# Entering a chunked recurrence without common waits, and splitting an output product around its end

## The chip, the cores and the metric

The kernel runs on one core of a Trainium2 chip. Its engines are TensorE (PE, matrix products; PEld is its weight load), VectorE (DVE), ScalarE (ACT), GpSimd (POOL) and SyncE (SP, which here only issues DMAs). Each has its own instruction stream, ordered by hand; streams meet through semaphores. The metric is the device time of one execution in microseconds (us), median of the runs; a kernel's profile comes from one further execution.

## The reference

Two blocks run one after the other on x (512 tokens x 1024 channels, fp32).

- **First block (RWKV-7).** x is normalised; six token-shifted mixes of it are multiplied by `w_in` into r, k, v, the gate g and two low-rank inputs. For each of 16 heads of width 64 a 64x64 state runs over the tokens: `S = S*w + (S @ -kk) (kk*a)^T + v k^T`, `y = S @ r`. y is normalised by head (mean and variance over 64), scaled, gets the bonus `sum(r*k*r_k) * v`, is multiplied by silu(g) and by `w_out`, and x is added: x1.
- **Second block.** Three vectors (shift, scale, gate) are computed from a condition by `w_ada` (1024 x 3072), for x and for a context of 256 tokens. x1 is normalised and modulated; products with `w_in_2` give a Fourier part and neighbourhood attention (8 heads, with the context's keys and values); both are gated, joined, multiplied by `w_out_2`, scaled and added to x1.

## The kernel before

The first block is computed in stages on PE. **Projections**: k, r, then a loop over eight channel tiles c (w, a and v, with the decays made on DVE and ACT), then eight products for g, `("g", c)`, each 24 matmuls of the split kind (three products of rounded halves, lines 518 to 520). **Recurrence**: tokens are cut in chunks of 64 (e = 0..7) and the channel tiles in two halves (hb = 0, 1); the 16 pairs in `ORDER` are the groups g = 0..15. One iteration of the loop over g works on several groups at once: `off_product` and `grow` double the inverted blocks of group g+1 and g (L679, L662 to L696), `turned` transposes (L662), `gram` makes the products of group g+2 (L647), `rhs_values`, `from_state`, `scan_sa` and `scan_out` (L708, L726, L742/L748, L760/L768) carry the state. Beside them stand the modulation's matrix-vector products with `w_ada` (`mods_here`: L780, L790), and from g = 9 the transposes of finished token tiles (`turn_y`: L807; each token tile j of 128 tokens has four pieces).

Before the recurrence, 16x16 diagonal blocks are inverted by forward substitution on DVE. `first_l` makes their products on PE, ACT copies them out (`copy_l`) and stores them in DRAM, `fetch_blocks(q)` (L1260) reads them back in another layout, `solve(b, part)` on DVE (L1601 to L1617; b = 0, 1; six parts of growing size) inverts, `store_inverse(b)` (ACT's queue, L1265) stores, and `fetch_inverse(b)` (SP's queue, L1120, eight DMAs) reads back; POOL's `expand(g)` (L2007) spreads them.

In the kernel before, DVE does all of both solves after the loop over c, with one buffer `XO` for both, so that the second waits for the store of the first. `gate(0)` to `gate(5)` (L1597, they free the banks of g) stand between the solve's parts, then `mask_gram(0)`, `gate(6)`, `gate(7)`. Then DVE, ACT and POOL each wait for the two others (`others_done`, `dve_phase` and so on) since the recurrence's buffers lie where the stage before had its own. PE does all eight g products, `gram(0)`, the first modulation product (whose bank 3 held g 7 and is freed by `gate(7)`), and the loop.

After the loop comes **y**: for each token tile j, DVE takes the mean off (`centre`, L1704 to L1706), ACT squares, DVE sums (L1757), ACT takes the root, DVE scales (L1760, L1761), PE transposes (`turn_y`), ACT applies the scale (`take_y`, L1350), DVE adds the bonus and gates (`finish_y`, L1713, L1715, which count up `y_gated`). PE then computes `project_y(t, h)` (token tile t, output half h; L524, 32 matmul records, two accumulations of 256 columns each). In order: tile 2's transposes, projections (0..2, 0), tile 3's transposes, (3, 0), (0, 1), the context's transposes (L896), (1, 1), (2, 1), x1's transposes for tile 0 (`turn_x1`, L879), (3, 1), tile 1's, and then the context's keys (first L524 after it).

On SP's queue, weights go through three buffers: block n is fetched when block n-3 is used. `fetch_inverse(0)` stands before block `split_g + 8`, `fetch_inverse(1)` before `split_g + 11`; x again (2 MB), the last block of `w_out` and the context follow when the recurrence has ended (L1142 to L1145; the context waits also for all of `y_gated`).

Lines that the steps touch: 

```
L524   last = mm(o, lhs(k), rhs(k), ...)          # accumulate
L780   last = mm(banks[MODS_BANK][...], SILC[:, k, :], w[:, k, :], ...)
L1613  own.own(TT(tmp, xo[...], LTB[b][...], MUL)) # solve
L1979  TT(WLO[...], WR[...], WHI[...], SUB)        # POOL splits a block of g's weights
```

## Time and profile before

| | us |
|---|---|
| median of 3 runs | 823.29 (821.58 to 829.12) |
| profiled execution | 819.92 |
| its span | 818.0 |
| PE busy | 762.1 (93%) |
| DVE, ACT, POOL busy | 446.0, 306.6, 172.3 |
| mean granted TensorE clock | 0.971 of full speed |

The span is the profile's own clock; about 1.9 us of the execution's time lie outside of it. In the page's second part each digit is a fortieth of the span (20.45 us). The granted clock has two levels, full (2.4 GHz) and half (1.2 GHz); a digit or figure between them is a mean over time.

### The profile page before, as it was taken

The page shows a single profiled execution, that of the slowest core. Times are in us where ns is not written, and L with a number is a line of the kernel's source. Part 1 is how long each engine was busy: PE and PEld are TensorE (multiplying, and loading weights), DVE is VectorE, ACT ScalarE, POOL GpSimd, SP SyncE. Part 2 cuts the span into 40 slices and gives each one's busy share as a digit, 9 for nine tenths or more (in the row PEclk, how much of TensorE's full clock was granted, in tenths as well). Part 3 has the DMA queues.
Part 4 walks back from the last instruction along what each step waited for, and adds up shares of the span by engine and source line. Part 5 has one row for each costly group of instructions (what it writes and reads, how often), then busy time and mean ns, then how long its engine had stood idle before and what let it go on. Part 6 is the DMA issues. An engine that isn't in the chain of part 4 may idle for free.

```text
span 818.0 us, 17638 instructions
## 1 busy us (share of the span) xinstructions
PE 762.1 (93%) x7612; PEld 618.4 (76%) x7612; DVE 446.0 (55%) x800; ACT 306.6 (37%) x638; POOL 172.3 (21%) x133
## 2 busy tenths in 40 slices
PE   3999999999998998988859899999999999999997
PEld 3588887777786787877847788877777777775697
DVE  5944635777879233556544123749655666754611
ACT  5534445566531122334331235523225453424200
POOL 2334330000342212324210000740000000002642
PEclk9999999999999599999978899999999999999999
DMA  7133233224458663310031134213302111231131
GB/s 245 30 100 103 78 100 107 78 79 91 123 126 217 141 220 125 128 55 4 4 121 35 52 103 112 62 53 92 113 3 76 52 53 53 62 107 52 51 105 52
DMA packets 116765, 72.83 MB, mean 89 GB/s; under 512 B 26832, under 2 KB 114128, under 8 KB 116688
## 3 DMA queue, kind: packets, MB, share of 16 engines
q1 hardware_dynamic: 98496, 65.12, 27.0%
q10 hardware_dynamic: 18192, 6.58, 3.3%
q8 instruction: 61, 1.00, 0.5%
q14 instruction: 16, 0.13, 0.1%
HBM read 64.35 MB, written 7.34 MB: 88 GB/s over the span
## 4 chain that ended last, share of the span: by engine, by line
PE 83%; DVE 9%; issue 3%; ACT 2%; DMA 2%; POOLq 0%; POOL 0%; SPq 0%; ACTq 0%; DVEq 0%
PE bank L524 21%; PE bank L983 9%; PE bank L518 6%; PE bank L520 6%; PE bank L519 6%; PE bank L647 2%; PE bank L1024 2%; PE bank L1007 2%; DVE arena L1613 2%; PE bank L780 2%; PE bank L696 2%; PE bank L543 2%; PE bank L679 2%; PE bank L1103 2%; PE bank L1105 2%
## 5 line engine op out<-in xcount | busy, mean ns | idle before, releaser
L524 PE MATMUL bank<-arena 128*128 128x256 f32 (+1 forms) x768 | 182.6, 396 | 4.5 <-DVE arena L1715 3.1
L524 PEld LDWEIGHTS bank<-arena 128*128 128x128 f32 x768 | 147.1, 194 | 38.4 <-issue 16.0
L1979 POOL TENSOR_TENSOR w_lo<-arena,w_hi 128x1024 fp32r<-128x1024 f32 x24 | 58.1, 2419 | 179.7 <-ACT w_hi L1196 179.7
L1196 ACT ACTIVATE w_hi<-arena 128x1024 fp32r<-128x1024 f32 x44 | 46.4, 1057 | 86.3 <-DMA arena<-w_in 84.6
L518 PE MATMUL bank<-x_hi,w_hi 128*128 128x512 f32 x192 | 76.4, 398 | 0.0
L520 PE MATMUL bank<-x_hi,w_lo 128*128 128x512 f32 x192 | 75.6, 394 | 0.0
L519 PE MATMUL bank<-x_lo,w_hi 128*128 128x512 f32 x192 | 75.3, 392 | 0.0
L518 PEld LDWEIGHTS bank<-x_hi,w_hi 128*128 128x128 f32 x192 | 36.1, 188 | 8.7 <-issue 0.8
L520 PEld LDWEIGHTS bank<-x_hi,w_lo 128*128 128x128 f32 x192 | 36.0, 188 | 8.4
L2076 POOL COPY arena<-arena 128x512 f32<-128x512 f32 x4 | 2.5, 614 | 189.2 <-DVE arena L1889 189.2
L519 PEld LDWEIGHTS bank<-x_lo,w_hi 128*128 128x128 f32 x192 | 36.1, 188 | 8.0
L983 PE MATMUL bank<-xn_hi,w_hi 128*128 128x512 f32 x96 | 39.6, 413 | 0.0
L983 PE MATMUL bank<-xn_hi,w_lo 128*128 128x512 f32 x96 | 38.0, 395 | 0.0
L983 PE MATMUL bank<-xn_lo,w_hi 128*128 128x512 f32 x96 | 37.9, 395 | 0.0
L1103 PE MATMUL bank<-w_out_hi,mix_hi 128*128 128x256 f32 x128 | 36.6, 286 | 0.2 <-DVE mix_lo L1946 0.2
L2007 POOL TENSOR_TENSOR arena<-arena 128x512 f32<-128x512 f32 x16 | 21.0, 1318 | 71.9 <-PE bank L742 56.1
L1557 DVE TENSOR_TENSOR x_lo<-arena,x_hi 128x512 fp32r<-128x512 f32 x24 | 21.6, 900 | 26.6 <-ACT x_hi L1200 26.5
L1105 PE MATMUL bank<-w_out_hi,mix_lo 128*128 128x256 f32 x128 | 36.0, 282 | 0.0
L1104 PE MATMUL bank<-w_out_lo,mix_hi 128*128 128x256 f32 x128 | 35.9, 281 | 0.0
L1868 DVE TENSOR_REDUCE arena<-bank 128x1 f32<-128x256 f32 x32 | 13.6, 424 | 40.0 <-PE bank L1000 40.0
L1489 ACT ACTIVATE arena<-arena 128x256 f32<-128x256 f32 x32 | 16.3, 509 | 50.8 <-DVE arena L1872 50.2
L1806 DVE TENSOR_TENSOR w_lo<-arena,w_hi 128x1024 fp32r<-128x1024 f32 x20 | 25.6, 1283 | 16.6 <-ACT w_hi L1196 16.6
(252 smaller groups left out, 1636.6 us busy)
## 6 DMA issues: line engine op xcount, KB each, us to landing
arena<-w_in SPq DMA_DIRECT2D x45, 512.0 KB, 3.9
arena<-w_ada SPq DMA_DIRECT2D x12, 1024.0 KB, 5.1
arena<-w_in SPq DMA_DIRECT2D x8, 1024.0 KB, 5.4
arena<-w_out SPq DMA_DIRECT2D x8, 1024.0 KB, 5.1
lt_dram<-arena ACTq DMA_DIRECT2D x16, 256.0 KB, 2.3
arena<-x SPq DMA_DIRECT2D x4, 512.0 KB, 5.6
arena<-x SPq DMA_DIRECT2D x1, 2048.0 KB, 7.6
out<-arena SPq DMA_DIRECT2D x8, 256.0 KB, 2.1
```

The source lines that it names most:

```text
L518: mm(o[:, :], w_hi[:, wk], x_hi, start=(k == 0), stop=False)
L519: mm(o[:, :], w_hi[:, wk], x_lo, start=False, stop=False)
L520: return mm(o[:, :], w_lo[:, wk], x_hi, start=False, stop=(k == KT - 1))
L524: last = mm(o, lhs(k), rhs(k), start=(k == 0), stop=(k == n - 1))
L983: last = mm(banks[5 + i % 2][:, :], w[slot][:, k * P:(k + 1) * P], v[k][:, :], start=(r == 0), stop=(r == 3 * KT - 1))
L1103: mm(oi, MXHI[k][:, at], W2HI[nb][:, wk], start=(k == 4), stop=False)
L1104: mm(oi, MXHI[k][:, at], W2LO[slot][:, wk], start=False, stop=False)
L1105: last = mm(oi, MXLO[k][:, at], W2HI[nb][:, wk], start=False, stop=(k == 3))
L1196: A(WHI[n % 3][:, :], WR[n % 3][:, 0:1024], ACT.Copy).then_inc(weights_rounded, 1)
L1557: TT(XLO[m][c][:, :], MIXES[m][:, c, :], XHI[m][c][:, :].bitcast(f32), SUB).then_inc(mixed, 1)
L1806: TT(WLO[n % 3][:, :], WR[n % 3][:, 0:1024], WHI[n % 3][:, :].bitcast(f32), SUB)\
L1979: TT(WLO[n % 3][:, :], WR[n % 3][:, 0:1024], WHI[n % 3][:, :].bitcast(f32), SUB)\
```

## The change

The three common waits go. g's products 6 and 7 get fixed banks (6 and 1) and `gram(0)` stands after product 5, `gram(1)` after product 6; the first modulation product moves into the loop. Groups 0 and 1 get `GM` buffers, and group 0 an `XS` buffer, in places that are free earlier (`GMG`, `XSG`), and each solve its own `XO` and `XTMP`. Parts 0 and 1 of `solve(0)` move into iterations 6 and 7 of the loop over c, with the fetch of the blocks one iteration earlier; the rest is put in a new order with the gates, and the stores and fetches of the inverses move with it.

At the other end, `project_y` is called by halves (t, h, i) of 16 matmul records. (0,0,0), (0,0,1) and (0,1,0) run in iterations 15, 16 and 17 of the loop, which now ends at 17 instead of 20. Tile 2's transposes come after it, in four banks instead of one; the projections before tile 3's transposes are (1,0), (1,1,0) and (2,0). The orders of ACT and DVE follow: tile 3's statistics go between tile 2's last steps, and x1's right halves are made before the context's norm. SP fetches the context without waiting for `y_gated`.

```diff
-        XO = arena[:, xi0 + 2560:xi0 + 3584].rearrange("p (q s a b) -> p q s a b", q=2, s=2, a=BLK)
-        XTMP = arena[:, xi0 + 3584:xi0 + 4096]
+        gt_at = xi0 + 4096
+        XO = [arena[:, at:at + 1024].rearrange("p (q s a b) -> p q s a b", q=2, s=2, a=BLK) for at in (gt_at + 3072, xi0 + 2560)]
+        XTMP = [arena[:, at:at + 512] for at in (gt_at + 2560, xi0 + 3584)]
...
+        XSG = [ROOT[0].rearrange("p (s c n) -> p s c n", s=2, c=4)] + [XS[:, g % 4] for g in range(1, GROUPS)]
+        GMG = [arena[:, at:at + 1024].rearrange("p (h c n) -> p h c n", h=2, c=4) for at in (lts_at, lts_at + 1024)] +\
+            [GM[g % 4] for g in range(2, GROUPS)]
...
-        def others_done(eng, n, mine):
-
-            for s in (act_phase, dve_phase, pool_phase):
-                if s is not mine:
-                    eng.wait_ge(s, n)
...
-                if i == 0 and g:
-                    pe.wait_ge(rhs_copied, g)
+                if i == 0:
+                    pe.wait_ge(rhs_copied, g) if g else stored(pe, ("g", 6))
...
+                o = out_bank((name, j, h), 3 if j < 2 else ((3, 0, 1, 2), (1, 2, 7, 4))[j - 2][piece])
...
-            gram(0)
-            mods_here(-1, 0)
+            for c in range(KT):
+                lo, hi = split_weights()
+                o = next_bank(("g", c)) if c < 6 else out_bank(("g", c), (6, 1)[c - 6])
+                for k in range(KT):
+                    if c == 0:
+                        pe.wait_ge(mixed, KT * 3 + k + 1)
+                    last = split_product(o, lo, hi, XLO[5][k][:, :], XHI[5][k][:, :], k)
+                full(last, ("g", c))
+                if c == 5:
+                    pe.wait_ge(kappa_ready, KT)
+                if c in (5, 6):
+                    gram(c - 5)
             for b in range(8):
-                if b not in (4, 5, MODS_BANK) and uses[b]:
+                if b not in (1, 4, 5, 6, MODS_BANK) and uses[b]:
                     pe.wait_ge(bank_free[b], uses[b])
+            wo = []
+            OUT_BANKS = {(0, 0): 4, (0, 1): 5, (1, 0): 6, (1, 1): 3, (2, 0): 0, (3, 0): 6}
+
+            def project_y(t, h, i):
+
+                pe.wait_ge(y_gated, 2 * (t + 1))
+                if not wo:
+                    wo.extend([weights() for _ in range(3)] + [WX])
+                if (h, i) == (1, 1):
+                    pe.wait_ge(wx_here, 16)
+                if i == 0:
+                    out_bank(("o", t, h), OUT_BANKS[t, h]) if (t, h) in OUT_BANKS else next_bank(("o", t, h))
+                b = where["o", t, h][0]
+                last = accumulate(banks[b][:, i * 256:(i + 1) * 256], lambda k: YG[t][:, k, :],
+                                  lambda k: wo[2 * h + i][:, k, :])
+                if i:
+                    last.then_inc(bank_full[b], 1)
+
             pe.wait_ge(y_zeroed, 1)
-            for g in range(-1, GROUPS + 5):
+            for g in range(-1, GROUPS + 2):
...
+                if g == GROUPS + 1:
+                    project_y(0, 1, 0)
...
+                if g in (GROUPS - 1, GROUPS):
+                    project_y(0, 0, g - GROUPS + 1)
...
-                if g + 2 < GROUPS:
+                if 0 <= g < GROUPS - 2:
...
-            for t in range(3):
-                project_y(t, 0)
+            for piece in range(4):
+                turn_y(2, piece)
+            for t, h, i in ((1, 0, 0), (1, 0, 1), (1, 1, 0), (2, 0, 0), (2, 0, 1)):
+                project_y(t, h, i)
             for piece in range(4):
                 turn_y(3, piece)
-            project_y(3, 0)
-            block_key[taken[0] - 2] = block_key[taken[0] - 1] = ("o", 3, 0)
-            project_y(0, 1)
+            for t, h, i in ((0, 1, 1), (1, 1, 1), (3, 0, 0), (3, 0, 1)):
+                project_y(t, h, i)
+            block_key[taken[0] - 3] = block_key[taken[0] - 2] = ("o", 3, 0)
+            turn[0] = 0
...
-            project_y(1, 1)
-            project_y(2, 1)
+            for i in range(2):
+                project_y(2, 1, i)
             turn_x1(0)
-            project_y(3, 1)
+            turn_x1(1)
+            for i in range(2):
+                project_y(3, 1, i)
             block_key[taken[0] - 1] = ("o", 3, 1)
-            turn_x1(1)
...
-                if n == split_g + KT + 3:
+                if n == split_g + KT + 1:
...
-                    sp.wait_ge(y_gated, 2 * NT)
...
-                if c in (5, 6):
-                    fetch_blocks(c - 5)
+                if c in (4, 5):
+                    fetch_blocks(c - 4)
...
-                if c == 3:
-                    store_inverse(0)
-            A(CST[:, 0:1], CST[:, 4:5], ACT.Copy).then_inc(act_phase, 1)
-            store_inverse(1)
-
-            others_done(act, 1, act_phase)
+                if c in (1, 4):
+                    store_inverse(c // 4)
...
+            square_y(3)
+            take_y(2, 0)
+            root_y(3)
+            take_y(2, 1)
...
-                    if b:
-                        dve.wait_ge(inv_out, 16 * b)
...
+                if c >= 6:
+                    solve(0, c - 6)
...
-            for b in range(2):
-                for part in range(6):
-                    solve(b, part)
-                    if part in (1, 2, 4):
-                        gate(3 * b + (1, 2, 4).index(part))
             def mask_gram(g, h):
                 o = arrived(dve, ("gram", g, h)).rearrange("p (c n) -> p c n", c=4)
-                free(TT(GM[g % 4][:, h], o, gram_mask.unsqueeze(1).broadcast_to([P, 4, 2 * CH]), MUL), ("gram", g, h))
-
-            for h in range(2):
-                mask_gram(0, h)
-            gate(6)
-            gate(7)
+                free(TT(GMG[g][:, h], o, gram_mask.unsqueeze(1).broadcast_to([P, 4, 2 * CH]), MUL), ("gram", g, h))
+
             free(nc.vector.tensor_copy(BON, arrived(dve, "bonus")[:, 0:64]), "bonus")
-            nc.vector.tensor_copy(CST[:, 1:2], CST[:, 5:6]).then_inc(dve_phase, 1)
-
-            others_done(dve, 1, dve_phase)
+            for part in range(2, 5):
+                solve(0, part)
+            gate(0)
+            solve(0, 5)
+            gate(1)
+            for i in range(3):
+                solve(1, 2 * i)
+                solve(1, 2 * i + 1)
+                gate(2 + i)
+            gate(5)
+            dve.wait_ge(inv_out[0], 16)
+            for i in range(2):
+                for h in range(2):
+                    mask_gram(i, h)
+                gate(6 + i)
...
+            centre(3)
+            finish_y(2, 0)
+            sum_y(3)
+            finish_y(2, 1)
+            norm_y(3)
...
-            make_x1(0, 1)
-            for t in range(1, NT):
+            norm_x1(0)
+            norm_x1(1)
+            make_x1(3, 0)
+            for t in (2, 3):
                 make_x1(t, 1)
-                norm_x1(t - 1)
-            norm_x1(NT - 1)
+                norm_x1(t)
...
+            arrived(pool, "bonus")
+            expand(0)
+            stored(pool, ("g", 6))
+            nc.gpsimd.memset(YL, 0.0).then_inc(y_zeroed, 1)
             arrived(pool, ("g", KT - 1))
-            expand(0)
-            others_done(pool, 1, pool_phase)
-            arrived(pool, "bonus")
-            nc.gpsimd.memset(YL, 0.0).then_inc(y_zeroed, 1)
```

## Rows read from the trace of the kernel before

**Rows 1.** The page, second part: granted clock of PE, in tenths.

```profile
PEclk9999999999999599999978899999999999999999
```

**Rows 2.** Busy time by stretch: us, each engine's busy (instructions), clock, DMA share, GB/s.

```profile
216.00:262.00 46.00, 45.67 (x224) 36.45 (x222) 39.20 (x72) 13.16 (x19) 18.46 (x9) 1.00 0.70 165
262.00:294.80 32.80, 27.64 (x528) 21.75 (x528) 10.88 (x27) 4.54 (x13) 7.68 (x10) 0.69 0.71 193
294.80:304.60 9.80, 9.27 (x284) 7.75 (x280) 3.04 (x8) 2.95 (x8) 2.08 (x3) 1.00 0.68 217
410.00:420.00 10.00, 6.67 (x137) 5.73 (x136) 4.00 (x8) 5.35 (x14) 0.39 (x1) 0.74 0.01 2
420.00:434.00 14.00, 6.59 (x37) 4.75 (x36) 6.06 (x7) 3.73 (x10) 3.05 (x3) 0.62 0.64 226
434.00:455.00 21.00, 21.00 (x96) 18.29 (x95) 7.41 (x10) 1.37 (x2) 0.00 (x0) 0.97 0.00 0
455.00:460.00 5.00, 1.91 (x17) 1.67 (x15) 3.43 (x5) 2.90 (x8) 0.00 (x0) 0.93 0.00 0
460.00:467.00 7.00, 6.97 (x18) 5.66 (x19) 0.00 (x0) 1.42 (x3) 0.00 (x0) 0.56 0.47 152
467.00:501.00 34.00, 34.00 (x174) 30.19 (x173) 6.43 (x12) 12.06 (x28) 0.00 (x0) 1.00 0.19 62
```

**Rows 3.** Timeline of PE at the entry: start, us, line; in brackets idle before, releaser.

```profile
260.57 1.10 PE L647 MATMUL bank<-arena 64*64 64x128 f32 x32
265.53 1.94 PE L780 MATMUL bank<-arena 128*32 128x256 f32 x16 [3.86 <-DVE arena L1597]
```

**Rows 4.** Timeline of DVE before the entry (start, us).

```profile
222.55 0.26 DVE L1615 TENSOR_REDUCE arena<-arena 128x14 f32<-128x98 f32 x1
...
232.39 2.63 DVE L1613 TENSOR_TENSOR arena<-arena 128x338 f32<-128x338 f32 x1
...
244.51 0.48 DVE L1607 MEMSET arena<- 128x512 f32 x1 [3.10 <-DMA inv_dram<-arena]
...
257.02 0.77 DVE L1613 TENSOR_TENSOR arena<-arena 128x338 f32<-128x338 f32 x1
...
265.44 0.14 DVE L1663 COPY arena<-arena 128x1 f32<-128x1 f32 x1
```

**Rows 5.** Timeline of POOL in the same stretch.

```profile
232.00 2.40 POOL L1979 TENSOR_TENSOR w_lo<-arena,w_hi 128x1024 fp32r<-128x1024 f32 x1 [1.74 <-ACT w_hi L1196]
```

**Rows 6.** Timeline of DVE at the head of iterations 6 and 7 over c.

```profile
195.86 0.43 DVE L1622 TENSOR_SCALAR arena<-arena 128x512 f32<-128x512 f32 x1 [2.33 <-ACT arena L1271]
...
206.91 2.19 DVE L1622 TENSOR_SCALAR arena<-arena 128x512 f32<-128x512 f32 x1 [3.10 <-ACT arena L1271]
```

**Rows 7.** Line 1260 (fetch of the blocks), issue of the first.

```profile
191.16 0.41 ACTq L1260 DMA_DIRECT2D arena<-lt_dram  x1
```

**Rows 8.** DMA issues of the whole span: count, KB each, us to landing (median).

```profile
arena<-w_ada SPq DMA_DIRECT2D x12, 1024.0 KB, 5.1
arena<-lt_dram ACTq DMA_DIRECT2D x4, 128.0 KB, 4.9
arena<-x SPq DMA_DIRECT2D x1, 2048.0 KB, 7.6
```

**Rows 9.** Timeline of SP at the entry: the second inverse's eight fetches.

```profile
267.39 6.91 SPq L1120 DMA_DIRECT2D arena<-inv_dram  x8
```

**Rows 10.** Timeline of PE at the recurrence's end and after it.

```profile
411.98 0.65 PE L696 MATMUL bank<-arena 64*64 64x32 f32 x16 [1.93 <-DVE arena L1673]
...
460.03 17.06 PE L524 MATMUL bank<-arena 128*128 128x256 f32 x64 [3.13 <-DVE arena L1715]
...
501.15 7.07 PE L524 MATMUL bank<-arena 128*128 128x256 f32 x32
```

**Rows 11.** Timeline of DVE at the recurrence's end: tiles 2 and 3, scaling.

```profile
422.29 2.64 DVE L1761 TENSOR_TENSOR arena<-arena 128x1024 f32<-128x1024 f32 x1
...
440.53 1.23 DVE L1761 TENSOR_TENSOR arena<-arena 128x1024 f32<-128x1024 f32 x1
```

More of the change, by code:

```diff
@@ L625, in _ @@
             first_l(KT - 1)
-            for c in range(KT):
-                lo, hi = split_weights()
-                o = next_bank(("g", c))
-                for k in range(KT):
-                    if c == 0:
-                        pe.wait_ge(mixed, KT * 3 + k + 1)
-                    last = split_product(o, lo, hi, XLO[5][k][:, :], XHI[5][k][:, :], k)
-                full(last, ("g", c))
-            pe.wait_ge(kappa_ready, KT)
             def gram(g):
@@ L1352, in take_y @@
                 free(ins, ("yT", j, h))
-            for g in range(-1, GROUPS + 5):
+            for g in range(-1, GROUPS + 2):
                 nxt, old = g + 1 < GROUPS, 0 < g <= GROUPS
@@ L1729, in _, with sum_y, norm_y @@
             heads_of = lambda a: a.rearrange("p (h n) -> p h n", n=HD)
-            for g in range(-1, GROUPS + 5):
+            def sum_y(j):
+                dve.wait_ge(gn_squared, j + 1)
+                nc.vector.tensor_reduce(stat(1, j), heads_of(SQ), AX.X, ADD).then_inc(gn_sums, 1)
+            def norm_y(j):
+                dve.wait_ge(gn_root, j + 1)
+                own.own(nc.vector.reciprocal(stat(2, j), stat(2, j)))
+                TT(heads_of(YT[j]), heads_of(YT[j]), bc(stat(2, j)), MUL).then_inc(y_normed, 1)
+            for g in range(-1, GROUPS + 1):
                 now, nxt, old = 0 <= g < GROUPS, g + 1 < GROUPS, 0 < g <= GROUPS
```

107 lines of the change are left out of this document (44 added, 63 removed).

## The prediction

> **What bounds the kernel.** The page comes first: PE is busy for 93% of the span, and its granted clock is full except in two places, the fourteenth fortieth (266 to 286 us) and the twenty-first to twenty-third (409 to 470) [rows 1]. These are the two ends of the recurrence, where the change works. The busy time by stretch says what they cost [rows 2]. Busy time times the granted clock is the time the same work would take at full clock. From 262.0 to 294.8, the first iterations, that is 27.64 x 0.69 = 19.1 us in 32.8. From 410 to 501 it is 4.9 + 4.1 + 20.4 + 1.8 + 3.9 + 34.0 = 69.1 us in 91. So 13.7 and 21.9 us are lost, part as idle time, part as half clock.
>
> Then the timelines, for what ends the waits. At the entry PE ends `gram(0)` at 261.7 and starts the first modulation product at 265.53; that takes 1.94 us, which is the half level. It waited 3.86 us for line 1597, the last `gate` on DVE [rows 3]. DVE is busy or waiting for its own store until 265.44 [rows 4], while PE was dense from 216 to 262 at full clock (45.67 of 46) [rows 2]. So DVE sets the entry, not the common waits: the others were done. At the other end PE waits 1.93 us before 411.98 and 3.13 before 460.03, each time for DVE, and within 420 to 434 it is busy for less than half [rows 2, 10].
>
> **The entry, part by part.** *DVE's load.* From 216.4, its first memset, to 265.4 DVE needs 49 us. It is busy for 39.2 of them up to 262 [rows 2] and for the 3.4 after. Two parts of `solve(0)` leave; part 1 ends with the reduce at 222.55 [rows 4], so they lasted 6.4 us. `mask_gram(1)` comes in (two of about 0.65). The store wait (3.10) goes, since each solve has its own `XO` [rows 4]. That makes 39.2 + 3.4 - 6.4 + 1.3 = 37.5 us: DVE could be ready at 254. But gates 6 and 7 need PE's last products, which end at about 257.5 and 263, so DVE has some 9 us in hand at g's last product, and from now on PE sets the time.
>
> *PE's stream.* Until 262 nothing of it is removed; `gram(1)`, which takes 1.10 us [rows 3], moves ahead of the loop. g 0 to 5 fill banks 2, 3, 4, 5, 0, 1, so `gram(0)` after product 5 needs gates 2 and 3 alone, due on DVE at about 243, when PE wants them at 250. `mask_gram(0)`, due about 255, is wanted by `gram(1)` at 257. The last gate falls at about 264.8, while PE is in `turned(0)` and the modulation product; `grow(0)` wants DVE at 265.4. PE should never pause for more than half a microsecond, so the clock stays full.
>
> *Its gain.* The work of 262.0 to 294.8 is 19.1 us at full clock. With the small waits of an iteration at full clock (9.27 busy of 9.80) [rows 2] it takes 20.2. **Gain 12.6 us**; I count 12.
>
> *What is moved to DVE's loop over c.* Part 0 and part 1 of `solve(0)`, about 2.7 and 1.7 us when nothing disturbs them, stand at the heads of iterations 6 and 7, where DVE waited for ACT for 2.33 and 3.10 us [rows 6]. Iteration 6 gets 0.4 us later, PE is on work that DVE gave it an iteration before. The blocks must have landed: the first fetch was issued at 191.16 in iteration 5 [rows 7] and would be in 4, the second in 5 at that place; 4.9 us to landing [rows 8] gives 196.1, where DVE arrives at 193.5 and spends 0.6 on memsets first. It may wait up to 2 us, on an iteration of 11 (195.86 to 206.91 [rows 6]). Between 0 and 2 us on PE; I take 0.3.
>
> *Queues.* SP issues the eight fetches of an inverse in 6.91 us [rows 9]. The second inverse now stands before the second modulation block. If it is solved at about 252 and stored by 255, SP is free at 262, and that block lands 5.1 us later [rows 8], at 267.5; PE wants it at about 268.5. Between 0 and 2 us, taken as 0, since the third block has more time.
>
> *A rule against it.* A solve step of 338 columns took 2.63 us at 232.39, and 0.77 at 257.02 when POOL was idle; a POOL split started at 232.00 and took 2.40 [rows 4, 5]. Eight such splits lie beside the solves, so DVE's budget above, which has the measured times, holds some 10 us of this already. The Trainium skill, "SBUF — State Buffer", "Who interferes with whom", says that the two engines share a pair of ports as an exclusive lock and the second fully blocks. The trace agrees; by that rule the moved parts can be hit too, which would add one split, 2.4 us, to DVE.
>
> **The exit.** All work from 410 to 501 is 69.1 us at full clock. The change does not remove any; it fills the recurrence's gaps. Walked through in the old time: (0,0,0) covers 410.0 to 413.5, when DVE's `mask_z` (due 411.9) and ACT's copy are awaited; (0,0,1) and (0,1,0) do the same for iterations 16 and 17, which end at 425.6 instead of 421.6. Tile 2's transposes have been ready since 419 and take 2.4 us in four banks. (1,0) and (1,1,0) then run to 438.4. Meanwhile tile 3 is centred (from 426), and tile 2 taken and finished: y_gated for (2,0) falls at about 437.3, only 1 us ahead. Tile 3 is scaled by 438.8 and PE turns it at 445.3. (0,1,1), (1,1,1) cover ACT's and DVE's last steps. x, `w_out`'s last block and the context, 4 MB, are asked for at 426; x alone takes 7.6 us [rows 8], all about 15; ACT needs the context by 443. `turn_x1` 0 and 1 have their norms ready before 470. The context's keys, at 501.15 before [rows 10], would start at 479.3. **Gain 21.9 us** at best. From it I take 2.5: handovers with margins of 1 to 4 us stand at (2,0), at tile 3's transposes and at the context, and the scaling of tile 2 took 2.64 us beside a POOL operation against 1.23 for tile 3 [rows 11]. **Net 19.4.**
>
> After 501 all engines keep their order, and the stage moves as a block; between 294.8 and 410 too.
>
> **Sum.** 819.92 - 12 + 0.3 - 19.4 = 788.8 us for a profiled execution. That execution was 3.4 us below the median of the three runs; half of this is put on top: **790**.
>
> **The rivals.**
>
> *DVE's chain stays late (0.14).* If locks and fetches cost DVE over 9 us more, `gram(1)` or the loop's first step pauses, and after a pause the clock was half from about 264.7 to 289 [rows 2]. For it: DVE is at 39.2 of 46 already. Against: the slack of 9. The entry then gives only about 3: 798 to 799.
>
> *The exit has a new pause (0.16).* (2,0) or tile 3 comes 2 us late; the clock falls as after the wait of 3.13 at 460.03 (0.56 for 7 us [rows 2], 3.1 us lost) or as at 415 to 434. Cost 5 to 9: 795 to 799. With the one before (0.02): 805.
>
> *Slower: half clock through the recurrence (0.04).* PE goes straight from dense products to many short ones with small waits. The first stretch needed 32.8 us for 19.1 of work, 1.72 to 1; at full clock it is 9.80 to 9.27, 1.06 to 1 [rows 2]. An iteration of 9.8 us would grow by 6.1. After five of them the gain of 31 is gone; from the seventh the kernel is slower by over 1%; all thirteen from 294.8 give about 868. Against: the same iterations ran at 1.00 with waits like these. The Trainium skill, "TensorE: Matmul & The Clock Gate", "A second HAM failure mode: psum-queue depth-cycling", tells of such a case, short pauses between groups of matmuls that make the clock swing; the trace has no swing in 294.8 to 304.6, and rule and rival would give the same time.
>
> *It does not do what it says (0.03).* The fills in the recurrence lengthen its own chain one for one, and the entry stays bound by DVE: 815 to 823.
>
> **Numbers.** The forecast holds with 0.61; its own range is 784 to 795. The full range is 782 to 805. About 1% (8 us) is what a measurement of this kernel can tell from none. Faster by more: 0.92 (0.61 + 0.14 + 0.16 + 0.02, less 0.01 for still larger pauses). Within 1%: 0.04 (these and the last rival). Slower: 0.04.
>
> **What would show it.** Entry: no PE wait over 1 us between 255 and 275, modulation products at half of 1.94 us from the first, iteration 2 begun at about 283 instead of 294.8; DVE's memset of `solve(1)` without a wait. Exit: three blocks of 16 L524 records among L726 and L742; clock 1.00 from 405 to 470 (old time); keys' first L524 20 to 22 us before the old distance. It would be wrong if the clock row shows a digit under 8 at either end, if DVE's waits at the heads of iterations 6 and 7 turn into waits for the fetch that reach PE, or if PE waits for ACT's `take_y` before (2,0).

## The result, and the profile after

The changed kernel takes 795.08 us in the median of four runs (794.85 to 796.46), the kernel before 822.43 on the same chip (821.36 to 829.12). The ratio is 0.969 (95% interval 0.965 to 0.973). The forecast was 790 us, in a range of 782 to 805. The profiled execution took 794.85 us, its span is 793.0 against 818.0: 25.0 us less where 31.1 were forecast (819.92 to 788.8).

The page comes first: the totals of PE and the row of the granted clock, the answer to [rows 1].

```profile
PE 754.0 (95%) x7612; PEld 610.9 (77%) x7612; DVE 442.4 (56%) x799; ACT 306.3 (39%) x637; POOL 171.2 (22%) x132
PEclk9999999999999889899999999999999999999999
```

The 5 at the fourteenth fortieth has become two digits of 8, and the digits 7, 8 and 8 at the recurrence's end are gone. A third 8, at the seventeenth (317 to 337 us), was a 9 before. Then the busy time by stretch, the answer to [rows 2] (same columns).

```profile
216.00:262.00 46.00, 44.38 (x246) 35.34 (x245) 40.73 (x64) 12.70 (x17) 18.71 (x9) 1.00 0.70 156
262.00:285.00 23.00, 22.16 (x427) 16.91 (x426) 4.60 (x13) 4.50 (x12) 5.39 (x7) 0.78 0.92 249
...
420.00:434.00 14.00, 14.00 (x87) 12.28 (x86) 6.56 (x9) 4.54 (x11) 2.90 (x3) 1.00 0.75 273
434.00:455.00 21.00, 21.00 (x107) 18.63 (x106) 10.74 (x19) 8.39 (x19) 0.00 (x0) 1.00 0.05 19
```

The exit is what was forecast and better: no idle time and full clock. The entry is not: 1.6 us idle ahead of 262, and a clock of 0.78 up to 285. PE's timeline at the entry shows where (idle time before an instruction and its releaser in brackets), against [rows 3]:

```profile
258.26 1.10 PE L635 MATMUL bank<-arena 64*64 64x128 f32 x32 [1.62 <-DVE arena L1660]
...
266.16 1.07 PE L770 MATMUL bank<-arena 128*32 128x256 f32 x16
...
268.98 1.06 PE L667 MATMUL bank<-arena 64*64 64x32 f32 x30 [0.68 <-DVE arena L1694]
...
271.29 1.89 PE L770 MATMUL bank<-arena 128*32 128x256 f32 x16 [0.16 <-DMA arena<-w_ada]
...
289.16 0.25 PE L667 MATMUL bank<-arena 64*64 64x32 f32 x2
```

Iteration -1 begins at 265.08, `gram(1)` waits 1.62 us for the first mask, the first modulation product has full clock (1.07 us), that at 271.29 has half (1.89). Iteration 2 begins at 289.16, forecast at 283, before at 294.81. ACT's timeline says what `gram(1)` waited for.

```profile
254.65 1.06 ACT L1203 ACTIVATE w_hi<-arena 128x1024 fp32r<-128x1024 f32 x1 [9.75 <-DVE arena L1625]
```

DVE's timeline of the same kernel, against [rows 4, 6]:

```profile
196.25 0.16 DVE L1621 TENSOR_TENSOR arena<-arena 128x2 f32<-128x2 f32 x1 [2.03 <-DMA arena<-lt_dram]
...
233.50 0.48 DVE L1615 MEMSET arena<- 128x512 f32 x1
...
253.57 0.64 DVE L1625 COPY arena<-arena 128x512 f32<-128x512 f32 x1
...
256.23 0.69 DVE L1607 SCALAR_TENSOR_TENSOR arena<-arena,bank 128x512 f32<-128x512 f32 x1 [1.43 <-ACT arena L1309]
256.83 1.28 DVE L1660 TENSOR_TENSOR arena<-bank,arena 128x512 f32<-128x512 f32 x2
```

The second solve begins without a wait (233.50; before, 3.10 us of it) and ends at 254.2, where "about 252" was forecast. ACT had stood 9.75 us in the wait for exactly this, ahead of its store of the inverse. Behind that wait stood the rounding of g's last weights and the tanh of gate 5, for which DVE then waited 1.43 us before the first mask. The SP queue, against [rows 9]:

```profile
259.39 6.04 SPq L1128 DMA_DIRECT2D arena<-inv_dram  x8
265.47 33.98 SPq L1144 DMA_DIRECT2D arena<-w_ada  x9
```

The second modulation block is asked for at 265.47, behind the eight fetches. At the other end, PE's timeline against [rows 10]:

```profile
406.44 3.72 PE L522 MATMUL bank<-arena 128*128 128x256 f32 x16
...
413.59 3.72 PE L522 MATMUL bank<-arena 128*128 128x256 f32 x16
...
418.36 3.62 PE L522 MATMUL bank<-arena 128*128 128x256 f32 x16
```

And DVE's two scalings, against [rows 11]:

```profile
414.11 1.23 DVE L1749 TENSOR_TENSOR arena<-arena 128x1024 f32<-128x1024 f32 x1
...
434.39 1.22 DVE L1749 TENSOR_TENSOR arena<-arena 128x1024 f32<-128x1024 f32 x1
```

The three halves of `project_y` stand as blocks of 16 records between the recurrence's last steps, and no record from 406 to 476 us has a wait in brackets. Both scalings take 1.2 us.

**Four stretches.** Every trace can be cut at three places: the start of iteration 2; the last `off_product` (L667, before L679); the first split product of the second block's keys (L516, before L518). For the changed kernel, the answer for L667 (first and last start, us):

```profile
L667 PE MATMUL bank<-arena x512: 211/219/313, 265.1 to 404.6; 64*64 64x32 f32 x171
```

Its first split product of the keys starts at 512.3.

All kernels of this study, cut in this way (us; the first column is the stretch up to iteration 2):

| kernel | to iteration 2 | middle | exit | rest | span |
|---|---|---|---|---|---|
| before | 294.8 | 113.3 | 130.9 | 279.0 | 818.0 |
| changed | 289.2 | 115.4 | 107.7 | 280.7 | 793.0 |
| e1 exit only | 295.9 | 116.2 | 107.7 | 279.0 | 798.8 |
| e2 entry only | 289.2 | 114.8 | 129.6 | 279.0 | 812.6 |
| e3 common waits back | 290.8 | 114.5 | 107.7 | 279.0 | 792.0 |
| e4 store wait back | 293.3 | 115.5 | 107.7 | 280.7 | 797.2 |
| e5 changed again | 292.6 | 115.2 | 107.7 | 280.7 | 796.2 |
| e6 store later | 290.9 | 120.3 | 107.7 | 279.0 | 797.8 |
| e7 filler | 291.4 | 121.3 | 107.7 | 279.1 | 799.5 |
| e8 both | 292.0 | 120.3 | 107.7 | 279.0 | 799.0 |
| e9 fetch later | 290.1 | 114.5 | 107.7 | 279.0 | 791.3 |
| e10 and filler | 291.6 | 118.6 | 107.7 | 280.7 | 798.6 |
| e11 and blocks later | 294.6 | 116.3 | 107.7 | 279.0 | 797.6 |
| e12 all four | 293.2 | 115.1 | 107.7 | 280.8 | 796.8 |

So the 25.0 us are 5.6 from the entry and 23.2 from the exit, less 2.1 in the middle and 1.7 in the rest. Each row is one execution, and some are quicker than their kernel's median: the traced execution of e2 took 814.54 us, 5.8 less than e2's median, that of e3 3.0 less. The stretches tell where a trace spends its time; what a kernel takes is told by the medians below.

### The profile page after: what moved, and what is told of

Same layout as the page of the kernel before. It is cut to its first block, busy times and chain, and to the rows that moved or that the text cites. A ratio compares the mean times of both kernels' runs of the same rounds, so it can differ in the third digit from the quotient of the medians.

```text
span 793.0 us, 17638 instructions
## 1 busy us (share of the span) xinstructions
PE 754.0 (95%) x7612; PEld 610.9 (77%) x7612; DVE 442.4 (56%) x799; ACT 306.3 (39%) x637; POOL 171.2 (22%) x132
## 4 chain that ended last, share of the span: by engine, by line
PE 83%; DVE 9%; DMA 3%; issue 3%; ACT 1%; SPq 1%; POOLq 0%; POOL 0%; ACTq 0%; DVEq 0%
PE bank L522 20%; PE bank L991 9%; PE bank L516 6%; PE bank L518 6%; PE bank L517 6%; DVE arena L1621 3%; PE bank L1032 2%; PE bank L1015 2%; PE bank L635 2%; PE bank L770 2%; PE bank L541 2%; PE bank L684 2%; PE bank L1111 2%; PE bank L1113 2%; PE bank L1112 2%
## 5 line engine op out<-in xcount | busy, mean ns | idle before, releaser
L522 PE MATMUL bank<-arena 128*128 128x256 f32 (+1 forms) x768 | 180.7, 393 | 1.4 <-DVE arena L1878 1.4
L522 PEld LDWEIGHTS bank<-arena 128*128 128x128 f32 x768 | 144.5, 191 | 35.0 <-issue 17.1
L516 PE MATMUL bank<-x_hi,w_hi 128*128 128x512 f32 x192 | 76.6, 399 | 0.0
L518 PE MATMUL bank<-x_hi,w_lo 128*128 128x512 f32 x192 | 75.6, 393 | 0.0
L516 PEld LDWEIGHTS bank<-x_hi,w_hi 128*128 128x128 f32 x192 | 36.1, 188 | 9.0 <-issue 1.2
L518 PEld LDWEIGHTS bank<-x_hi,w_lo 128*128 128x128 f32 x192 | 36.0, 188 | 8.3
L1820 DVE RECIPROCAL arena<-arena 128x512 f32<-128x512 f32 (+1 forms) x12 | 33.8, 2816 | 1.1 <-ACT arena L1438 1.0
```

The source lines that it names most:

```text
L516: mm(o[:, :], w_hi[:, wk], x_hi, start=(k == 0), stop=False)
L518: return mm(o[:, :], w_lo[:, wk], x_hi, start=False, stop=(k == KT - 1))
L522: last = mm(o, lhs(k), rhs(k), start=(k == 0), stop=(k == n - 1))
L1820: own.own(nc.vector.reciprocal(r, r))
```

## The experiments

Three groups of four, each on one chip beside the kernel before; the changed kernel's 0.969 is from a group of its own. The kernel before had a median of 825.41 us beside e1 to e4, 825.14 beside e5 to e8 and 822.73 beside e9 to e12; a ratio is to that.

### One half of the change at a time

**e1, exit only.** The entry of before, and of the diff the calls of `project_y` by halves and what belongs to them:

```diff
+                if g == GROUPS + 1:
+                    project_y(0, 1, 0)
...
+                if g in (GROUPS - 1, GROUPS):
+                    project_y(0, 0, g - GROUPS + 1)
```

> The kernel before with the second half of the change alone (the first block's output product in halves around the recurrence's end, loop ended at GROUPS + 1), the entry as before. My theory: the two halves of the change simply add, and the exit is worth what the two traces show between the end of the last state's reading and the keys' first product, 22.3 us, less about 0.9 us that comes back behind it: 21.4 us less than before, about 801 us, ratio 0.974, and from 20 us before the keys' first product back to the recurrence the clock at 1.00. Rival: part of the gain hangs on the entry's state (the banks or the clock that it leaves), then less than 18 us, over 804 us.

Measured: 802.01 us, ratio 0.973 (0.969 to 0.976). The exit takes 107.7 us, as in the changed kernel.

**e2, entry only.** The other hunks of the diff; the bank counter is set so that the exit finds its old banks.

```diff
+            turn[0] = (turn[0] + 2) % 6
             pe.wait_ge(y_zeroed, 1)
-            for g in range(-1, GROUPS + 2):
+            for g in range(-1, GROUPS + 5):
```

> The changed entry alone, with the exit as before. My theory: iteration 2 begins 5 to 6 us earlier, the recurrence gives some 2 us of it back (half clock in 317 to 322 us), so 3.6 us less than before, about 819 us, ratio 0.9956. Rival, my prediction as it stands on record: 12 us, 810 us, ratio 0.985. Second rival: the 2 us are given back for a reason that has nothing to do with the entry (then they are missing here, 5.6 us less, 0.993).

Measured: 820.38 us, ratio 0.994 (0.992 to 0.996); iteration 2 at 289.2, as in the changed kernel. The same stretch of PE in e1 (us, PE busy, clock, DMA share, GB/s):

```profile
405.00:460.00 55.00, 53.71 (x599) 1.00 0.22 78
```

And in e2:

```profile
405.00:460.00 55.00, 41.02 (x317) 0.81 0.22 74
```

What follows: the halves add, as far as can be told. 0.973 x 0.994 = 0.967, the whole has 0.969 (0.965 to 0.973). My number of 12 us for the entry is refuted: the entry alone gives 0.6%, some 5 us.

### Did the common waits cost anything?

**e3.** `others_done` returns on the three engines, nothing is moved back.

```diff
             expand(0)
+            others_done(pool, 1, pool_phase)
             stored(pool, ("g", 6))
             nc.gpsimd.memset(YL, 0.0).then_inc(y_zeroed, 1)
```

> The changed kernel with the three common waits put back where the engines stand (ACT behind the last gate's tanh, DVE behind gate 7, POOL behind the expansion of group 0), all other moves kept. Theory A: the waits themselves had a price, by the one that they put on POOL: its clear of YL starts at 259.34 us in the changed kernel and would have to wait for DVE's gate 7, which ends at 266.5; PE's loop waits for that clear and could start only at about 267.3 instead of 265.08, ACT's first copy of the turned keys 0.3 us later: 2 to 4 us slower than the changed kernel, 797 to 799 us, ratio to before 0.969 to 0.972. Theory B: the moves (Gram products between the gate's last products, solves spread into the loop over c) are all that counts, and the waits are free: under 0.5 us, ratio as the changed kernel's.

Measured: 796.85 us, ratio 0.966 (0.961 to 0.971); that can't be told from the changed kernel's 0.969. The trace has the mechanism, with its size. POOL's timeline in e3:

```profile
265.94 0.52 POOL L2071 MEMSET arena<- 128x512 f32 x1 [7.11 <-DVE arena L1687]
```

PE's:

```profile
266.79 0.60 PE L674 MATMUL bank<-arena 64*64 64x32 f32 x14 [2.37 <-issue]
```

POOL's clear waits for DVE's last gate, PE for the clear, 2.37 us. Iteration 2 begins 1.6 us later than in the changed kernel, although the whole stage stands 0.9 us earlier in e3 (PE's last block of L582, L589 in e3, starts at 212.79 against 213.73); counted from there it is 2.5 us, within theory A's 2 to 4. In the whole that is no more than what the middle and the rest differ by from trace to trace. So taking the waits out is worth about 2.4 us in the place where they stood, and the total doesn't show it.

### Has DVE slack?

**e4.**

```diff
                 if part == 0:
+                    if b:
+                        dve.wait_ge(inv_out[0], 16)
                     own.own(nc.vector.memset(xo, 0.0))
```

> The changed kernel in which DVE waits for the first inverse's store again before it begins the second solve (the second buffer stays, only the wait returns). It tests the slack of some 9 us that my prediction gave DVE between the second solve and the Gram masks. The store is issued at 232.9 us and such stores take 4.5, so DVE would stand from 233.5 to 237.4. Theory A (no slack: the solve's end holds ACT in its store wait, then the gates, the masks and PE): the loop starts 2 to 4 us later (2 if one of the three lock collisions beside POOL's splits, of 2.2 us each, falls into the wait), 797 to 799 us. Theory B (9 us of slack, as predicted): no change, 795 us.

Measured: 799.11 us, ratio 0.969 (0.966 to 0.972). DVE's timeline in e4:

```profile
238.31 0.48 DVE L1617 MEMSET arena<- 128x512 f32 x1 [4.41 <-DMA inv_dram<-arena]
...
258.87 0.69 DVE L1607 SCALAR_TENSOR_TENSOR arena<-arena,bank 128x512 f32<-128x512 f32 x1 [1.43 <-ACT arena L1309]
```

PE's:

```profile
260.90 1.23 PE L635 MATMUL bank<-arena 64*64 64x128 f32 x32 [2.06 <-DVE arena L1662]
```

DVE stands 4.41 us; gate 5 comes 2.6 us later (258.87 against 256.23), since the first of the meetings with POOL's splits falls into the wait. PE now waits at both Gram products (1.74 us ahead of the first, at 251.96, for DVE's gate), the clock is 0.80 from 262 to 270, and the loop starts 4.1 us later (269.2). There is no slack: theory A, at the upper end of its range. The total doesn't separate it from the changed kernel, which ran in another group (ratio 0.969 both); the verdict rests on the traces.

### The changed kernel a second time

**e5.** No edit.

> The changed kernel itself, for a second profile. Five traces so far have 279.0 or 280.7 us from the keys' first split product to the end, and 113.3 to 116.2 us from the start of iteration 2 to the last off-diagonal product, without order by what was changed. Theory A: both are chance of one execution, so this profile may show 279.0 where the first had 280.7 and a middle that differs by up to 2 us, while the loop's start (265.1), iteration 2 (289.2) and the exit (107.7 us from the last off-diagonal product to the keys' first split product) repeat within 0.3 us. Theory B: they belong to the kernel: 280.7 and 115.4 again.

Measured: 800.49 us, ratio 0.972 (0.965 to 0.979). The middle and the rest came out as in the first trace (115.2 and 280.7): theory B by the letter. The loop's start (265.3) and the exit repeat; iteration 2 doesn't. PE's timeline in e5:

```profile
274.21 1.93 PE L770 MATMUL bank<-arena 128*32 128x256 f32 x16 [2.86 <-DMA arena<-w_ada]
```

SP's:

```profile
262.03 5.90 SPq L1128 DMA_DIRECT2D arena<-inv_dram  x8
267.97 30.49 SPq L1144 DMA_DIRECT2D arena<-w_ada  x8
```

The store of the inverse landed after 7.5 us here, after 5.1 in the first trace. All that stands behind it on SP's queue moves, and PE waits 2.86 us for the second modulation block, for which it had waited 0.16.

The two traces part long before that, at g's first products. The first line is from e5, the second from the first trace:

```profile
217.17 0.63 PE L516 MATMUL bank<-x_hi,w_hi 128*128 128x512 f32 x1
...
217.52 0.39 PE L516 MATMUL bank<-x_hi,w_hi 128*128 128x512 f32 x1
```

In both PE had just waited for DVE in the last pass over c (1.15 us in e5, 1.06 in the first trace; 0.57 in the kernel before). In e5 the clock is half for some 3 us behind it, in the first trace it stays full. PE then runs 1.5 us late, and so does SP, which fetches a block when PE has used an older one. SP in e5 and in the first trace:

```profile
253.42 0.96 SPq L1144 DMA_DIRECT2D arena<-w_ada  x1
...
251.73 0.80 SPq L1144 DMA_DIRECT2D arena<-w_ada  x1
```

The store of the inverse follows this 1 MB block by 1.1 us in e5 and by 2.5 in the first trace. Over the 12 traces with the new entry, in groups, the store lands the later the closer it follows: 7.3 to 7.7 us at 0.8 to 1.2 us of distance (e3, e5, e7, e10, e11), 6.6 at 1.7 (e9), 5.0 to 5.6 at 2.1 to 2.8 (first trace, e2, e6, e8, e12), 3.2 at 4.3 (e4). No run sets this distance alone. The 1.5 us of half clock are in eight of the 12 (e3, e5 to e8, e10 to e12), after waits of 1.04 to 1.80 us, and missing in four (first trace, e2, e4, e9), after 0.98 to 1.29: no edit and no size of the wait sorts them.

It also decides the pause ahead of `gram(1)`, which is 0.39 us in e5. The mask comes at the same time (257.11 against 256.83), so PE waits the less by what it lost at half clock, and the loop starts at 265.3 against 265.1.

### The two pauses and the clock

**e6.**

```diff
-                if c in (1, 4):
+                if c in (1, 5):
                     store_inverse(c // 4)
```

> The changed kernel with ACT's store of the second inverse behind the rounding of the gate's last weights and the sixth gate's tanh instead of ahead of them. In the changed kernel ACT stands 9.75 us in that store's wait, DVE's gate 5 waits 1.43 us for ACT and PE 1.62 us for DVE's first mask. Theory A (that order is the cause of PE's pause, and no more): gate 5 doesn't wait, the first mask starts at 255.4 instead of 256.8, PE's pause is under 0.4 us, iteration 2 begins 1.3 us earlier (287.9). Theory B: the rounding set free also frees POOL's split of the same weights, which then falls beside DVE's second solve; each such meeting made one DVE product 1.7 us longer (2.33 us for 242 elements, 0.67 for 288), so the mask starts at 257 as before and nothing is won, 0 to 0.4 us slower.

Measured: 800.26 us, ratio 0.971 (0.965 to 0.977). POOL's timeline in e6:

```profile
250.69 2.59 POOL L2001 TENSOR_TENSOR w_lo<-arena,w_hi 128x1024 fp32r<-128x1024 f32 x1 [3.52 <-ACT w_hi L1203]
```

DVE's:

```profile
251.65 2.45 DVE L1621 TENSOR_TENSOR arena<-arena 128x450 f32<-128x450 f32 x1
...
256.55 1.27 DVE L1660 TENSOR_TENSOR arena<-bank,arena 128x512 f32<-128x512 f32 x2
```

Theory B: the wait for ACT is gone, but the split that it held back now meets the solve's last product (2.45 us, 0.95 in e5). The mask starts 0.6 us earlier than in e5 (257.11), but the whole stage stands 0.7 us earlier in e6 (PE's last L582 block at 212.99 against 213.66): nothing is won. e7, where the store stands as before and the stage as in e6 (213.00), has the mask at 256.49.

**e7.**

```diff
+                if g == 0:
+                    for _ in range(2):
+                        mm(banks[7][:, 256:512], ident, AR[:, 0, 0, 0:256], start=True, stop=True,
+                           skip_group_check=True)
                 if nxt:
                     off_product(g + 1, 0)
```

> The changed kernel with two extra TensorE products of 128x256 fp32 into an unused half of bank 7 between the iterations -1 and 0 of the recurrence, where PE has its pause of 0.98 us at 268.0 us (their results are not read). The granted clock is 1.00 up to 271, 0.50 from there to 281. Theory A: that pause is what costs the clock; with the filler in it the clock stays 1.00, the stretch 271 to 281 takes half of its time, iteration 2 begins 4 to 5 us earlier (284 to 285 us), the whole about 790.5 us. Theory B: it is not the pause but the earlier one (1.62 us at 256.6) or the small products themselves (64x32 and 64x64 on 64 rows): clock as before, iteration 2 at 289.2, the whole unchanged.

Measured: 798.64 us, ratio 0.969 (0.963 to 0.976). **e8**, both edits:

> Both of the last two edits. Under theory A of both: no PE pause over 0.5 us from 255 to 285, clock 1.00 throughout, iteration 2 at 283 us, 789 us. If the clock falls still, neither pause is its cause. If it stays at 1.00 here and fell with the filler alone, the earlier pause is (or both together are) the cause.

Measured: 801.43 us, ratio 0.974 (0.967 to 0.980). Neither tells anything of the clock. The pause ahead of iteration 0 (0.68 us by its bracket; the expectation's 0.98 counts from the last record's start) was filled, and PE then stood for the second modulation block, 2.66 us in e7 and 2.83 in e8; the clock fell behind that wait.

### The fetches behind the blocks

**e9.**

```diff
-                if n == split_g + KT + 1:
+                if n == split_g + KT + 3:
                     fetch_inverse(1)
```

> The changed kernel with SP's eight fetches of the second inverse two blocks of the stream later, as in the kernel before (behind the second and third block of the modulation's weights). The second profile of the changed kernel has PE standing 2.86 us at 271.3 us for the second of these blocks, which SP could only ask for at 268.0, after the store (7.5 us to landing there) and the fetches (5.9 us); the first profile has the same wait at 0.16 us, with the store landed in 5. Theory A: my prediction missed that the fetches now stand ahead of that block; with them behind it the block is asked for at 259 to 262, the wait is gone on any chip, iteration 2 begins 3 us earlier than in the second profile, and still with half clock in 271 to 281 (289 us). Theory B: the block is late by the traffic, not by its place in the queue: the wait stays over 1.5 us, or the fetches are now late for group 3 and PE stands there.

Measured: 795.24 us, ratio 0.965 (0.961 to 0.969), the lowest of all, with an interval that overlaps the changed kernel's. PE's timeline in e9:

```profile
258.60 1.10 PE L635 MATMUL bank<-arena 64*64 64x128 f32 x32 [1.61 <-DVE arena L1660]
...
269.32 1.06 PE L667 MATMUL bank<-arena 64*64 64x32 f32 x30 [0.67 <-DVE arena L1694]
...
271.41 1.82 PE L770 MATMUL bank<-arena 128*32 128x256 f32 x16
```

Theory A: no wait for `w_ada` at all, half clock from 272 to 280 as in the changed kernel.

**e10**, this and the filler:

> The same with the two extra products of 128x256 fp32 in PE's pause of 0.98 us between iterations -1 and 0. The filler alone told nothing of the clock, since PE stood 2.66 us for the modulation's weights right behind it. Now both pauses are closed. Theory A (pauses cost the clock): 1.00 from 265 to 285, iteration 2 at 284 to 285, 4 to 5 us less than without the filler. Theory B (the small products of these iterations don't hold it): the clock falls all the same, iteration 2 as in the run without filler.

Measured: 802.08 us, ratio 0.974 (0.969 to 0.978): slower than e9 by 6.8 us in the medians; the intervals touch (0.9692 and 0.9694).

**e11**, the fetches and:

```diff
-                if c >= 6:
-                    solve(0, c - 6)
+                if c == 7:
+                    solve(0, 0)
+                    solve(0, 1)
```

> The fetches later, and both first parts of the first solve in the last pass of DVE's loop over c instead of one each in the last two. In the changed kernel DVE stands 2.0 us there for the blocks that come back from memory, and PE 1.1 us behind it. DVE's chain from the second solve on has no slack (the store wait given back moved the loop's start by its whole 4.1 us). Theory A: the slack is missing back to the loop over c as well, so the 2 us that DVE no longer stands move the loop's start 1 to 2 us earlier. Theory B: PE's 1.1 us are all that counts, DVE then does the same work later and meets POOL elsewhere: 0 to 1 us.

Measured: 798.66 us, ratio 0.970 (0.963 to 0.976). Theory A falls. DVE no longer waits for the blocks, it waits in the same place for ACT (2.63 us, so the 2.0 us had cost nothing), and has the more to do in iteration 7; PE's wait there is 1.80 us instead of 1.1, and the loop starts at 266.1, 0.7 us later than in e9. PE's timeline at the entry in e11:

```profile
259.29 1.10 PE L635 MATMUL bank<-arena 64*64 64x128 f32 x32 [0.48 <-DVE arena L1661]
...
270.02 1.06 PE L667 MATMUL bank<-arena 64*64 64x32 f32 x30 [0.68 <-DVE arena L1695]
```

Two windows of PE in e9 (us, busy, clock, DMA share, GB/s):

```profile
272.00:280.00 8.00, 8.00 (x112) 0.50 0.73 124
282.00:290.00 8.00, 6.74 (x174) 1.00 1.10 350
```

The same in e10:

```profile
272.00:280.00 8.00, 6.31 (x188) 1.00 0.78 142
282.00:290.00 8.00, 8.00 (x120) 0.50 1.06 335
```

And in e11:

```profile
272.00:280.00 8.00, 7.30 (x202) 1.00 0.66 82
282.00:290.00 8.00, 5.38 (x84) 0.50 1.07 347
```

e9 has half clock first and full after it, e10 and e11 the other way round. In e11 the pause of 0.68 us is there, and the clock holds; so that pause alone isn't the cause. What differs from e9 is the earlier one: 0.48 us instead of 1.61 (0.46 in e10). No edit made it short: the filler stands behind it. It is short because PE came to it 1.5 us later, after the half clock at g's first products that e10 and e11 have and e9 hasn't. So these three traces are no test of the pauses; they show what follows a short one and a long one. And the clock that was kept is lost again behind a new wait. PE's timeline in e10:

```profile
281.55 1.93 PE L770 MATMUL bank<-arena 128*32 128x256 f32 x16 [3.18 <-DMA arena<-w_ada]
```

SP's:

```profile
265.33 10.44 SPq L1131 DMA_DIRECT2D arena<-inv_dram  x8
275.81 8.10 SPq L1147 DMA_DIRECT2D arena<-w_ada  x4
```

At full clock PE is at the fourth block by 278, and SP asks for it only at 275.8, after eight fetches that take 10.4 us right behind a block of 1 MB (6.04 in the changed kernel, 6.91 before [rows 9]). In e11 PE waits 5.25 us for the same block, and iteration 2 begins at 294.6. **e12**, all four edits:

> All four edits: the second inverse's fetches later, the first solve's two parts together, ACT's second store behind the sixth gate's tanh, the filler in PE's pause. If they add: loop's start 263 us, no PE wait over 0.7 us up to iteration 2; with the clock held (theory A of the filler) iteration 2 at 282.5 and 788 us on the first chip; without it 287 and 792 us.

Measured: 800.99 us, ratio 0.973 (0.967 to 0.978). The clock is full from 265 to 280, PE waits 3.46 us for the same block, iteration 2 begins at 293.2. They don't add.

## Why the prediction was right, and where it was not

**The whole.** Right in sign, size and range; 5 us under. The entry gave 6.4 less than the 12 counted, the stretches "that move as a block" took 3.8 more, and the exit gave 3.8 more than its net 19.4. That the total came within 5 us is in part luck: the exit's surplus stood against the entry's shortfall. Of its signs two went against it: PE did wait over 1 us between 255 and 275 (1.62), and DVE's wait at the head of iteration 6 became one for the fetch, which reached PE with half a microsecond.

**The exit: the mechanism held, the deduction for handovers was too much.** 21.9 us at best, 2.5 taken off; measured are 23.2 against the trace of before and 21.9 against e2. None of the margins failed: no pause from 406 to 500, clock 1.00. The 2.64 us scaling that I held against it [rows 11] stood beside a POOL operation (2.07 us from 421.78); in the changed kernel POOL's (1.91 us from 422.75) falls beside neither scaling (1.23 and 1.22). The stretch is 107.7 us in all 12 traces with the new exit: with no wait in it and full clock, it has one length.

**The entry: 12 us predicted, 5.6 measured, 2.2 in the second trace.** The loop's start was put at 263 and came at 265.1, iteration 2 at 283 and came at 289.2. By steps:

1. *The first mask, "due about 255"*. This step failed, by two terms. The first is DVE's budget. I took 6.4 us off for the two parts that leave, and priced the same parts at 2.7 + 1.7 = 4.4 us undisturbed: the 2.0 between is, but for a few tenths, the meeting with POOL's split (a product of 18 columns took 2.42 us at 217.94 before). The split stayed where it was and met another product of the solve instead:

```profile
218.41 2.39 DVE L1621 TENSOR_TENSOR arena<-arena 128x200 f32<-128x200 f32 x1
```

And 37.5 us were busy time, without some 2 us of gaps of 0.03 between the instructions. The busy time came out at 40.7, the solve ended at 254.2 instead of 252, and some 5 us of masks and gates stood behind it, so that DVE, without any further wait, would have been ready at about 259, not 254. The second term is ACT, where I had not asked what was queued behind the moved store: a wait of 9.75 us with the last rounding and a tanh behind it, for which DVE waited 1.43. The masks ended at 258.1, PE was there at 256.6. The "9 us in hand" counted to g's last product, where they were of no use; at the first mask there are none (e4). e6 shows that it isn't mended by another order on ACT alone, since the rounding sets POOL's split free and that meets DVE's solve. This is the lock that the prediction named, from the other side. The Trainium skill, "SBUF — State Buffer", "Who interferes with whom", says that a DVE instruction with two inputs in SBUF contends with a GpSimd instruction that reads SBUF, over a port pair that is an exclusive lock; e6's rows agree: the solve's product takes 2.45 us beside a split of 2.59, against 0.95 alone.
2. *"PE should never pause for more than half a microsecond, so the clock stays full"*. It paused 1.62 us at 256.6 and 0.68 us at 268.3, and had half clock from 271.3 to 281.2, which costs 9.9 / 2 = 4.9 us. These are the larger part of what is missing. The pauses themselves are not: with 0.39 us in place of 1.62 e5 starts the loop no earlier. In the five traces with a first pause of 1.5 us or more (changed, e2, e3, e4, e9; in e3 it stands right ahead of the loop) the second modulation product had half clock (1.77 to 1.89 us); in e10, e11 and e12, with 0.33 to 0.48, it had full clock (1.07). In e5 to e8 the wait for the block came first. That is eight traces to one side, not a test that sets the pause by itself. The three with the short pause also had the half clock at g's first products, and four of the five others hadn't; only e3 had both that and a long pause (2.37), and its clock fell. So that the pause costs the clock is likely, not shown.
3. *SP's queue, "between 0 and 2 us, taken as 0"*. 0.16 us in the first trace, 2.86 in the second: the bound was too narrow. It had the solve done at 252 and the store landed at 255, 3 us; the store was issued at 254.2 and took 5.1 in the first trace, and over the 12 traces with the new entry 3.2 (e4) to 7.7 (e7), by how closely it followed a block of 1 MB (e5 above). Behind it is the step that the prediction left out. With the clock held, PE runs into the weight stream: wherever the eight fetches stand, one block of `w_ada` is behind them. So the 4.9 us of half clock weren't to be had by the edits tried: e10 kept the clock there, then waited 3.18 us and had half clock from 281 to 293, and began iteration 2 at 291.6, e9 at 290.1. Of the other 5.8 us between their traces 4.1 lie in the middle and 1.7 in the rest. Fetches on another queue, which would free SP, weren't tried.
4. *The blocks for the first solve, "may wait up to 2 us", 0.3 taken*. The wait came (2.03 us), and the PE block that DVE's iteration 7 holds up started 0.45 us later than before (213.73 against 213.28), near the 0.3 taken. e11 removed the wait and gained nothing. Not priced was what PE's own wait there, now 1.0 us or more, may set off: 1.5 us at half clock in eight of 12 traces, which the mask hides and SP's queue doesn't (e5).

**"After 501 all engines keep their order, and the stage moves as a block; between 294.8 and 410 too".** Not to the microsecond. The rest has two lengths, 279.0 (9 of 14 traces, with one of 279.1) and 280.7 (5, with one of 280.8). Changed kernel and e9 reach it at the same time (512.3) and come to the same wait at the same time, and part there. PE in the changed kernel:

```profile
724.98 15.67 PE L522 MATMUL bank<-arena 128*128 128x512 f32 x32 [1.42 <-DVE arena L1878]
```

PE in e9:

```profile
724.99 13.97 PE L522 MATMUL bank<-arena 128*128 128x512 f32 x32 [1.42 <-DVE arena L1878]
```

The clock is 0.91 over the next 20 us in the first, 1.00 in the second. Nothing in the program differs from 512.3 on. The Trainium skill, "TensorE: Matmul & The Clock Gate", "What's actually happening", says that the same kernel starts with more or fewer products at half clock from one run to the next; these two rows show such a difference in the middle of a kernel. The middle has 113.3 to 121.3 us, by where the clock dips. In the first trace PE paused 1.65 us ahead of 315.57 and had half clock for nearly 7 us behind it: this is the third 8 in the page's row. It did so in e2 to e5 too (115.5 us or less), while e9 paused 1.93 us there and kept full clock. e6, e7, e8 and e10, with a middle of 118.6 to 121.3 us, had half clock from about 307 to between 314 and 318, after pauses of 0.85 to 1.13 and of 0.98 us; e9, with 0.86 and 0.98 there, kept full clock. What decides it is open.

**The rivals.** The first one (DVE's chain stays late, 0.14) is what the entry did: 1.6 us of pause ahead of the loop and half clock, with a gain of 3 priced and 5.6 measured. Its condition, DVE over 9 us late, wasn't needed: 2 us and ACT's 1.43 were enough. The exit's pause and "does not do what it says" didn't come; of the half clock through the recurrence only short spells did, that of 316 to 323 us above all. The whole stayed at the edge of the forecast's own range (784 to 795), because the exit gave 2.5 to 3.8 us more than counted.

## What to carry to other kernels

When a wait is moved up an engine's queue, count what stands behind it on that engine, and who needs that: here a store's wait on ACT held back a tanh, by it DVE's mask, and by it PE, whose clock was half for 10 us soon after. When work is moved out of a list, take off its undisturbed price: what it lost to another engine stays behind for its successor. Filling gaps of PE with work that is ready (the projection's halves) paid in full. Where PE kept its clock ahead of a stretch that is fed by DMA it did not pay: PE only reached the next block sooner, stood there, and lost the clock in that place. And before two traces are compared at the place of an edit, look for where they first part: here it was 50 us ahead of it, and the kernel was the same.

## What the runs showed of the hardware

- Small fetches block a queue. Eight of 64 KB take SP 5.8 to 7.8 us to issue, and 9.3 to 10.6 us when they start right behind a load of 1 MB (e9 to e12).
- The same 512 KB store from SBUF to DRAM landed in 3.2 us (e4), 5.1 us (the changed kernel's first trace) and 7.5 us (e5), issued 4.3, 2.5 and 1.1 us after a 1 MB load from another queue.
- A DVE product with two SBUF inputs takes 2.45 us beside a POOL split of 2.59 us, and 0.95 alone (e6, e5). If the DVE instruction that met the split is moved away, the next one meets it.
- After one and the same wait of 1.42 us, ahead of 32 dense products, the clock held in e9 and not in the changed kernel: 13.97 and 15.67 us.
